# Expert stage: the prompt's rows of eight experts gathered, transposed and turned back together as 128 rows

## The reference, cut to what matters

```python
D_MODEL = 1024
SEQ = 128
DEC_SEQ = 1024
N_EXPERTS = 16
EC_FACTOR = 2
D_EXPERT = 2816

def expert_choice_ffn(h, router, e_gate, e_up, e_down):
    b, t, _ = h.shape
    cap = EC_FACTOR * t // N_EXPERTS
    aff = jax.nn.softmax(jnp.einsum('btd,de->bte', h, router).astype(jnp.float32), axis=-1)
    gate, idx = lax.top_k(jnp.swapaxes(aff, 1, 2), cap)
    bidx = jnp.arange(b)[:, None, None]
    xe = h[bidx, idx]
    hid = jax.nn.silu(jnp.einsum('becd,edf->becf', xe, e_gate)) * jnp.einsum('becd,edf->becf', xe, e_up)
    ye = jnp.einsum('becf,efd->becd', hid, e_down) * gate[..., None].astype(h.dtype)
    return jnp.zeros_like(h).at[bidx, idx].add(ye)
```

## Time and profile before

| | |
|---|---|
| median of 3 runs | 3868.48 us (3867.92 to 3871.03) |
| the profiled execution | 3860.96 us, of which the span from first to last instruction 3859.2 us |
| mean granted TensorE clock | 0.967 of full speed |
| PE busy | 3562.1 us (92%) |
| DVE busy | 1231.4 us (32%) |
| ACT busy | 671.1 us (17%) |
| POOL busy | 192.0 us (5%) |
| `topk` | 1574.0 to 1639.4 us |
| `experts` | 1640.6 to 3831 us |
| `final` | 3831.5 us to the end |

### The profile page before, as it was taken

The page is one execution under the profiler, slowest core; times in us unless marked ns, Lnnn a source line. Parts: engine busy times, 40 slices in busy tenths (PEclk is TensorE's granted clock), DMA queues, the critical chain, the costliest instruction groups (busy, mean ns, idle before and its releaser), DMA issues. The chain is left out here.

```text
span 3859.2 us, 81746 instructions
## 1 busy us (share of the span) xinstructions
PE 3562.1 (92%) x37038; PEld 3101.1 (80%) x37038; DVE 1231.4 (32%) x3103; ACT 671.1 (17%) x1677; POOL 192.0 (5%) x150
## 2 busy tenths in 40 slices
PE   5899899999899979289999999999999999999995
PEld 2387685959555545189999999999999999999995
DVE  3376767777444443701111111111111111111112
ACT  2323324242144532100000000000000000000001
POOL 0010101010000000000000000000000000000000
PEclk7899999999999999589999999999999999999997
DMA  7200000000121022098887878788787878878773
GB/s 323 61 16 10 15 5 20 4 19 4 27 79 31 18 72 94 21 354 292 274 266 263 267 259 273 261 273 268 265 267 258 273 262 269 268 268 269 258 251 110
DMA packets 498393, 664.38 MB, mean 172 GB/s; under 512 B 31183, under 2 KB 437095, under 8 KB 494975
## 3 DMA queue, kind: packets, MB, share of 16 engines
q1 hardware_dynamic: 492238, 640.23, 49.5%
q0 software_dynamic: 5632, 18.88, 1.9%
q10 hardware_dynamic: 176, 0.05, 0.0%
HBM read 630.70 MB, written 28.36 MB: 171 GB/s over the span
## 5 line engine op out<-in xcount | busy, mean ns | idle before, releaser
L2094 PE MATMUL bank<-e_hid,e_wd 128*128 128x144 f32 x5632 | 760.1, 288 | 0.0
L2082 PE MATMUL bank<-e_xT,e_wg 128*128 128x144 f32 x5632 | 749.5, 286 | 1.0 <-ACT e_xT L2136 1.0
L2082 PE MATMUL bank<-e_xT,e_wu 128*128 128x144 f32 x5632 | 748.1, 286 | 0.0
L2082 PEld LDWEIGHTS bank<-e_xT,e_wg 128*128 128x128 f32 x5632 | 715.5, 190 | 1.0 <-issue 1.0
L2094 PEld LDWEIGHTS bank<-e_hid,e_wd 128*128 128x128 f32 x5632 | 710.5, 190 | 5.6
L2082 PEld LDWEIGHTS bank<-e_xT,e_wu 128*128 128x128 f32 x5632 | 714.4, 190 | 0.0
L2179 DVE TENSOR_TENSOR e_tm<-bank,e_sg 128x144 f32<-128x144 f32 x352 | 108.3, 308 | 1853.0 <-ACT e_sg L2143 1853.0
L2143 ACT ACTIVATE e_sg<-bank 128x144 f32<-128x144 f32 x352 | 102.2, 290 | 1998.4 <-PE bank L2082 1998.4
L532 PE MATMUL bank<-hT_x,wblk 128*128 128x512 f32 (+1 forms) x672 | 237.5, 511 | 14.5 <-DMA wblk<-in_w_in 8.5
L532 PEld LDWEIGHTS bank<-hT_x,wblk 128*128 128x128 f32 x672 | 114.1, 197 | 130.4 <-issue 112.4
L727 PE MATMUL bank<-r_TW,r_X 64*64 64x64 f32 x2880 | 167.5, 220 | 4.3 <-DVE r_X L1198 1.3
(11 more groups left out here) (324 smaller groups left out, 3469.9 us busy)
## 6 DMA issues: line engine op xcount, KB each, us to landing
e_wg<-in_e_gate SPq DMA_DIRECT2D x176, 1024.0 KB, 5.5
e_wu<-in_e_up SPq DMA_DIRECT2D x176, 1024.0 KB, 8.1
e_wd<-in_e_down SPq DMA_DIRECT2D x176, 1024.0 KB, 11.0
h_wmod<-in_w_mod SPq DMA_DIRECT2D x24, 1024.0 KB, 17.1
wblk<-in_w_in SPq DMA_DIRECT2D x22, 512.0 KB
h_x<-in_x_sample SPq DMA_DIRECT2D x8, 512.0 KB, 6.6
wo<-in_w_out SPq DMA_DIRECT2D x2, 2048.0 KB, 11.6
o_x<-in_x_sample SPq DMA_DIRECT2D x8, 512.0 KB, 4.2
```

The costliest lines, as they stand in the source:

```text
L2082: last = nc.tensor.matmul(bank[6 + b % 2][:, j * TOK:(j + 1) * TOK], w[s][:, k, f], xT[e % 2][:, k, :], start=(k == 0), stop=(k == KD - 1))
L2094: last = nc.tensor.matmul(bank[k // PER_BANK][:, c:c + TOK], wd[s][:, b % DUO, k * P:(k + 1) * P], hid[:, b % 2, :], start=(b == 0 and k % ...
```

## The change

In `topk` the prompt's two rounds come first. As soon as they are done, SP writes the prompt's lists to HBM and reads them back as `idxq` and `gateq`, [128, 2]: column g has the lists of eight experts, one entry per partition. In `experts` the prompt's rows are gathered as 128 rows for experts 0 to 7 and again for 8 to 15, turned by 8 transpositions of 128 rows each time, and kept in `xpT`. For each expert, DVE copies its 16 columns from `xpT` to `xT`. On the way back, DVE collects each expert's 16 columns of `yT` in `ypT`; after experts 0 to 7 and again after 8 to 14 they are turned together, scaled together, and POOL then adds them expert by expert, each scatter waiting for the one before. Expert 15's prompt rows are done by themselves at the end.

The core of the difference:

```diff
-                for at, n, col, cap in ((0, NS, 0, CAP), (NS, NP, CAP, CAPP)):
+                for at, n, col, cap in ((NS, NP, CAP, CAPP), (0, NS, 0, CAP)):
+                    if at == 0:
+                        dve.sem_inc(prompt_ok, 1)
...
+            @block.sync
+            def _(sp):
+                sp.wait_ge(prompt_ok, 1)
+                sp.dma_start(K.dram["idxq"][:, :], idx[:, CAP:TOK]).then_inc(listed, 16)
+                sp.dma_start(K.dram["gateq"][:, :], val[:, CAP:TOK]).then_inc(listed, 16)
+                sp.wait_ge(listed, 32)
+                for dst, name in ((K.idxq, "idxq"), (K.gateq, "gateq")):
+                    sp.dma_start(dst[:, :], bass.AP(tensor=K.dram[name].tensor, offset=0, ap=[[1, P], [P, 2]]),
...
-                            sp.dma_start(gt2p[:, :], mod_row(K, GT2, 1, CAPP)).then_inc(rows, 16)
+                            sp.dma_start(gt2p[:, :], mod_row(K, GT2, 1)).then_inc(rows, 16)
...
+                def gather_prompt(g):
+                    pool.indirect_dma_start(out=xp[:, :], out_offset=None, in_=K.dram["h2p"][:, :],
+                                            in_offset=bass.IndirectOffsetOnAxis(ap=K.idxq[:, g:g + 1], axis=0))\
+                        .then_inc(xp_in, 16)
+
+                def scatter_prompt(e):
+                    if e:
+                        K.hold(pool, scp, 16 * e)
+                    rows = part(e) if e < NE - 1 else slice(0, CAPP)
...
                 gather(0)
+                gather_prompt(0)
                 K.hold(pool, x_ps, 1)
                 gather(1)
+                K.hold(pool, xp_ps, 2)
+                gather_prompt(1)
                 for e in range(NE):
                     if e + 2 < NE:
                         K.hold(pool, x_ps, e + 2)
                         gather(e + 2)
-                    K.hold(pool, s_ok, 4 * e + 4)
+                    for g, (first, last) in enumerate(GROUP):
+                        if e == last + 1 or (e == last and last == NE - 1):
+                            K.hold(pool, sp_ok, 2 * g + 2)
+                            for i in range(first, last):
+                                scatter_prompt(i)
+                    K.hold(pool, s_ok, 2 * e + 2)
...
+                K.hold(pool, sp_ok, 6)
+                scatter_prompt(NE - 1)
+                K.hold(pool, scp, 16 * NE)
+                K.hold(pool, sc, 16 * NE)
...
-                    nc.tensor.transpose(bank[b][:, c:c + CAP], xe[:, k * P:(k + 1) * P], K.ident[:, :])
-                    last = nc.tensor.transpose(bank[b][:, c + CAP:c + TOK], xp[:, k * P:(k + 1) * P],
-                                               K.ident[0:CAPP, 0:CAPP])
...
+                        if e == GROUP[0][1] - 1 and b in (2, 3, 4, 5, 9, 10, 11, 12):
+                            prompt_token(1, b - 2 if b < 6 else b - 5, 5)
+                        for g, (first, last) in enumerate(GROUP):
+                            if e == last and b in (4, 5, 6, 7, 10, 11, 12, 13):
+                                prompt_output(g, b - 4 if b < 8 else b - 6)
                 for k in range(KD):
                     output(NE - 1, k)
+                pe.wait_ge(sp_ok, 4)
+                for k in range(KD):
+                    output_last_prompt(k)
...
+                    V.tensor_copy(xT[e % 2][:, HALF:KD, 0:CAP], bank[4][:, :].rearrange("p (k t) -> p k t", t=P))
+                    dve.wait_ge(xp_ok, 2 * (e // 8) + 2)
+                    V.tensor_copy(xT[e % 2][:, :, CAP:TOK], xpT[:, :, part(e)]).then_inc(xv_ok, 1)
...
+                def collect(e):
+                    dve.wait_ge(ya_ok, e + 1)
+                    dve.wait_ge(yv_ok, e + 1)
+                    if e == GROUP[1][0]:
+                        dve.wait_ge(yp_ps, 2)
+                    V.tensor_copy(ypT[:, :, part(e)], yT[:, :, CAP:TOK]).then_inc(yc_ok, 1)
```

More of the change, by code:

```diff
@@ L1997, in experts @@
         yT = sb("yT", [P, KD, TOK])
-        ye, yp = sb("ye", [P, D]), sb("yp", [CAPP, D])
+        ypT = sb("ypT", [P, KD, P])
+        ye, yp = sb("ye", [P, D]), sb("yp", [P, D])
         gt2 = sb("gt2", [P, D])
-        gt2p = sb("gt2p", [CAPP, D])
+        gt2p = sb("gt2p", [P, D])
         bank = K.bank
@@ L2007, in experts, with part @@
         d_ps, ya_ok, yv_ok, y_ps, s_ok = (sem(n) for n in ("down_psum", "yT_act", "yT_dve", "y_psum", "y_scaled"))
-        sc = sem("scattered")
+        sc, scp = sem("scattered"), sem("prompt_scattered")
+        xp_in, xp_ps, xp_ok = sem("xp_in"), sem("xpT_psum"), sem("xpT_ok")
+        yc_ok, yp_ps, sp_ok = sem("ypT_ok"), sem("yp_psum"), sem("yp_scaled")
+        GROUP = ((0, 8), (8, 15))
+        HALF = KD // 2
+        def part(e):
+            return slice((e % 8) * CAPP, (e % 8 + 1) * CAPP)
         with nc.Block() as block:
@@ L2044, in _ @@
                         gather(e + 2)
-                    K.hold(pool, s_ok, 4 * e + 4)
-                    if e:
[L2047 to L2052, removed]
+                    for g, (first, last) in enumerate(GROUP):
[4 more added lines that the diff above has]
+                    K.hold(pool, s_ok, 2 * e + 2)
+                    if e:
+                        K.hold(pool, sc, 16 * e)
+                    pool.indirect_dma_start(out=K.dram["ffn"][:, :],
+                                            out_offset=bass.IndirectOffsetOnAxis(ap=K.idx[:, e:e + 1], axis=0),
+                                            in_=ye[:, :], in_offset=None, compute_op=ALU.add).then_inc(sc, 16)
+                K.hold(pool, sp_ok, 6)
+                scatter_prompt(NE - 1)
+                K.hold(pool, scp, 16 * NE)
+                K.hold(pool, sc, 16 * NE)
             @block.tensor
@@ L2207, in _ @@
                         hidden(e, b)
+                        if e and b == YT + 2:
+                            collect(e - 1)
                         if e and b == YT + 5:
@@ L2211, in _ @@
                             scaled(e - 1, 1)
+                        if e == GROUP[0][1] - 1 and b in (8, 15):
+                            prompt_tokens(1, b // 15, 5)
+                        for g, (first, last) in enumerate(GROUP):
+                            if e == last and b in (9, 15):
+                                prompt_scaled(g, b // 15)
                         if b == XT + KD + 1 and e + 1 < NE:
```

96 lines of the change are left out of this document (74 added, 22 removed).

## The result

The changed kernel takes 3805.24 us in the median of 4 runs (3804.65 to 3808.65), against 3869.18 us for the kernel before in the same comparison: ratio 0.9836, 95% interval [0.9819, 0.9853], 63.9 us less. The forecast was 3813 with a range of 3803 to 3832. The profiled execution took 3805.23 with a span of 3803.5; the forecast for that span was 3803.6.

What follows compares the result with a forecast made beforehand. PE was taken to bound the expert stage, giving back every removed distance. Loop 52.6, start 0 and end 3 sum to 55.6 us, taken off the 3868.48 median: 3812.9, rounded to 3813, range 3803 to 3832.

Steps and rivals of the forecast that it cites:

- The loop: Expert loop on PE: transpositions removed on the way in and back, less those added, gain 52.6 us.
- The pair's price of 0.35: Steps with `token`: each removed 16-row `xp` transposition gives 0.35 us (0.46 less 0.11), 42 us over 120.
- Rival B: Way in: removing a small transposition saves only its 0.16 us slot, neighbours' excess stays; 3836 us, chance 0.07.
- The price by 16 of 128 columns: Way in: a small transposition priced by columns alone, 0.014 us; time 3853 us, chance 0.01.
- The start: Start of the experts, up to PE's first product: no gain taken, with -2 to +3 us.
- Rival D: Start of experts: first group's gather lands more than 8 us late, sharing engines with weights; 3821 or more, chance 0.02.
- The end: Expert stage's end, from last product to next stage: sample scatter and last prompt scatter go out earlier, gain 3 us.
- D: Moment when the expert stage's last product ends, 3811.2 us in the kernel before; end-of-stage forecasts count from it.
- The chain of seven: POOL's seven last-group prompt scatters ahead of the last sample scatter: hidden if each round stays under about 6.1 us.
- R: Round from one prompt scatter to the next, landing plus 0.9: taken as 5.5 us, bounds 2.2 and 10.
- Rival A: Expert stage's end: POOL sees landings late, so the seven last-group scatters are exposed; 3840 us at 10 us rounds, chance 0.12.
- rival C: Expert stage: denser work makes the chip grant less clock; 3884 us at a granted clock of 0.967, chance 0.03.

Runs made afterwards that it cites:

- in_only: Changed kernel with only the way in batched for eight experts; way back, scatters and scaling as in the kernel before: 3819.47 us, ratio 0.9874.
- xp_full_rows: Kernel before, with prompt rows in a 128-partition tile turned by a 128-row product with the identity's first 16 columns: 3848.18 us, ratio 0.9948.
- second pair: Kernel before and changed kernel, both unedited, each traced once more: medians 3867.14 and 3804.89 us.
- xp_together: Kernel before, with the eight 16-row transpositions per expert standing together behind the eighth of 128 rows: 3834.28 us, ratio 0.9918.
- first_in_topk: Changed kernel, with the first group's prompt rows gathered, turned and copied already inside the top-k stage: 3803.53 us, ratio 0.9842.

## Why the prediction came out as it did

The mechanism and the loop's sum held; the forecast was 8 us too high, within its range. That the forecast for the profiled span, 3803.6, met the measured 3803.5 is luck: the change gave 60.6 us after the top-k, five more than forecast, and that execution reached the top-k 4.8 us later than the one from which the forecast was taken.

*The loop.* Forecast 52.6, measured 53.1. The bound was as read: PE gives every removed distance back, and SP still waits for PE, 1517.3 us in all. The pair's price of 0.35 is what in_only shows (41.7 + 0.9 for the eight added, over 120, is 0.355). Its reason, the 16-row load between 128-row ones, was argued from the "issue" wait of the earlier trace rows. The runs show it for the greater part: a second 16-row one costs 0.063, the same eight standing together lose 30.7 of the 42, and with 128 rows the 0.09 of excess on `xe` is gone. The 0.10 behind the pair is not peculiar to 16 rows: 0.08 of it stays behind two short products of 128 rows. Rival B is out: in the changed kernel neither excess is left (0.11 and 1.97). The price by 16 of 128 columns, 0.014, was wrong by 25 times; the Trainium skill's floor of about 25 ns between starts (TensorE: Matmul & The Clock Gate, "Wait — 56ns, not 53.3ns?") isn't contradicted by the steps with `token`, where the closest starts are 0.03 us apart (the two short products of xp_full_rows), but it doesn't price the change of rows.

*The start.* This term failed in size: "I take 0", measured 2.8 (2.6 in the second pair). I had the prompt's rows landing 2 us late; they were there when PE had turned `xe`, so PE began 1.1 us sooner than before and waited once. The first product is 1.8 us sooner. The rest, 1.0, is the clock: the first 32 products took 5.6 us instead of 6.6, at a granted clock of 0.70 in that stretch instead of 0.60 (windows of before and of after; columns as in the earlier trace rows):

```profile
1656.15:1662.73 6.58, 6.58 (x32) 6.58 (x33) 0.00 (x0) 1.20 (x1) 1.65 (x2) 0.60 1.06 382
...
1659.24:1664.87 5.63, 5.63 (x32) 5.63 (x33) 0.00 (x0) 0.00 (x0) 0.12 (x1) 0.70 1.06 401
```

The clock rose to its upper level 5.3 us behind the first product in before and 3.4 in after. Batching isn't needed for this: the same 32 take 5.6 in xp_together too, and 6.6 in first_in_topk. What makes the rise come sooner wasn't tried. Rival D is out: PE did not wait for the prompt's rows.

*The end.* Forecast 3, measured 4.4. The sample's scatter went out at D + 3.9 as forecast, the last one at D + 5.75, where I had 6.3. The interval behind it was 10.1, not 11.1, and why it was shorter isn't shown. The final stage, which the change doesn't touch, took 0.4 less (27.3 instead of 27.7).

*The chain of seven.* Hidden, as forecast, with more room than I gave it: a round is 3.9 us, the landing alone 3.1, where I took 4.6 from a scatter that stood behind one of 128 rows (the last scatter of the changed kernel, in the same place, again takes 4.6). R by the fit of the Trainium skill (DMA: Bandwidth & Descriptors, "Anatomy of one DMA — SWDGE (gpsimd) path") was an estimate of 4.3, nearer to the 3.9 than mine of 5.5 by the row. Rival A's premise, a POOL that sees landings late, is out: in the chain POOL goes on 0.8 us behind a landing, so the 6.5 us behind the last landing of before (5.5 in after) are not in such a wait. What they are wasn't tried. The rounds of the eight scatters in iteration 9 took 4.0 to 8.2 us with the weights streaming, and POOL then had 33.9 us to spare.

*The clock (rival C).* At 1.00 in the loop as before; no sign of it.

*The base.* Terms of 60.6 instead of 55.6 explain 5 of the 8 us. The other 3 are the spread of the medians of few executions, by what the table shows: the parts that the change doesn't touch differ by up to 9.3 us from one trace to the next, and the first trace of before had the shortest stretch ahead of the top-k of all twelve.

## What to carry to other kernels

Ask of a small operation on a saturated TensorE what it does to its neighbours: the distance from the last full-size start before it to the second group behind it, less what the same stretch takes without it, is its price; its own slot or its columns are not. If a few transpositions with fewer rows must be made, put them next to each other: reordering alone gave 31 of the 42 us here, without a new buffer, gather or list. Short products of 128 rows are no way round it: they leave 0.22 of the 0.35. And put a chain of dependent scatters where an engine's long work covers it; the same seven cost nothing ahead of the last product and 29 us behind it.

## What was not expected

- A transposition of 16 rows between operations of 128 rows costs 0.35 us, and behind another of 16 rows 0.063 us: 0.09 of the 0.35 stand in front of it, 0.16 are its own slot, 0.10 stand behind.
- Two short products of 128 rows and 16 moving columns cost 0.22 us, as much as two transpositions with 128 moving columns: in this place the columns made no difference. Their weight loads of 128x128 stand 0.11 us apart without a gap and may set it (not tried apart).
- A scatter-add of 16 rows of 4 KB that has the DMA engines to itself lands 3.1 us after its issue and is followed by the next 3.9 us after it (one round of six took 5.7); with weights streaming the rounds are 4.0 to 8.2 us.
- The attention stage, which nothing here touches, is longer in the trace in which its granted clock is lower; with the stages before it, it lets the top-k start anywhere within 9.3 us over twelve traces.
